# Two blocks of a sequence model: a weight remainder on VectorE, modulation loads two turns later, modulation sums behind the softmax divisions

## What is computed

```python
def first_block(x, ...):
    proj = rms_norm(x, g_mix) @ w_in                       # 1024 -> 4352
    xa = depthwise_conv(u_a, conv_a_w, conv_a_b, 2)
    y_a = (rglru(xa, forward) + rglru(xa, backward)) @ p_a # 1280 wide
    y_b = (block_diag(multiscale_pool(u_b), w_pool, b_pool) * pool_scale) @ p_b
    x = x + (gates_a * y_a + gates_b * y_b) @ w_out
    up = depthwise_conv(rms_norm(x, g_ffn) @ w_up, conv_f_w, conv_f_b, 1)
    x = x + (gelu(up[..., :2816]) * up[..., 2816:]) @ w_down
    return rms_norm(x, g_final)

def second_block(x, c, ...):
    mod = silu(c) @ w_mod + b_mod                          # 1024 -> 6 x 1024
    shift1, scale1, gate1, shift2, scale2, gate2 = split(mod, 6)
    u = rms_norm(h, norm1_g) * (1 + scale1) + shift1
    xs, q, ckv, qi, ki, wi, ga, gb = split_cols(u @ w_in)
    y_ssm = s5_branch(xs, ...)         # state space scan, gelu, gated product
    y_att = dsa_branch(q, ...) @ w_attn_proj  # 8 heads, top-128 keys per query
    h = h + gate1 * ((sigmoid(ga) * y_ssm + sigmoid(gb) * y_att) @ w_out)
    u2 = rms_norm(h, norm2_g) * (1 + scale2) + shift2
    h = h + gate2 * ((silu(u2 @ w_gate) * (u2 @ w_up)) @ w_down)   # 2816 wide
    return rms_norm(h, final_g)
```

## Time and profile before

| | |
|---|---|
| time, median of three runs | 1467.01 us (1464.62, 1467.01, 1467.63) |
| the profiled execution's own time | 1468.92 us |
| its span, first to last instruction | 1467.6 us |
| TensorE busy | 1450.2 us, 99% |
| VectorE busy | 888.4 us, 61% |
| ScalarE busy | 787.8 us, 54% |
| GpSimd busy | 173.0 us, 12% |
| mean granted clock of TensorE | 0.996 of full speed |
| HBM read and written | 177.62 and 17.83 MB |

### The profile page before, as it was taken

The page is one execution under the profiler, slowest core; times in us unless marked ns, Lnnn a source line. Parts: engine busy times, 40 slices in busy tenths (PEclk is TensorE's granted clock), DMA queues, the critical chain, the costliest instruction groups (busy, mean ns, idle before and its releaser), DMA issues.

```text
span 1467.6 us, 18322 instructions
## 1 busy us (share of the span) xinstructions
PE 1450.2 (99%) x6992; PEld 1190.5 (81%) x6992; DVE 888.4 (61%) x1623; ACT 787.8 (54%) x1082; POOL 173.0 (12%) x183
## 2 busy tenths in 40 slices
PE   9999999999999999999999999999999999999998
PEld 8887788888888788888888877776878888888887
DVE  6879854365595859476477668847876343333332
ACT  6699898745665556543444565586356222222221
POOL 1111111111111111100002421121010000000000
PEclk9999999999999999999999999999999999999999
DMA  8876888899999798883348666895467433333321
GB/s 260 190 193 161 205 190 200 193 318 292 305 262 273 183 243 224 207 259 122 108 165 280 198 165 167 205 337 201 141 155 222 150 107 109 87 101 100 101 72 58
DMA packets 86935, 275.42 MB, mean 188 GB/s; under 512 B 10096, under 2 KB 14448, under 8 KB 86848
## 3 DMA queue, kind: packets, MB, share of 16 engines
q1 hardware_dynamic: 62256, 190.95, 38.8%
q0 software_dynamic: 21344, 77.67, 27.8%
q10 hardware_dynamic: 3248, 5.64, 1.1%
HBM read 177.62 MB, written 17.83 MB: 133 GB/s over the span
## 4 chain that ended last, share of the span: by engine, by line
PE 86%; ACT 5%; DVE 5%; DMA 2%; issue 1%; SPq 0%; DVEq 0%; ACTq 0%
PE ps L725 27%; PE ps L728 26%; PE ps L726 26%; DMA wlo<-raw 2%; ACT whi L1222 1%; ACT wlo L1231 1%; DVE pl_f L2119 1%; ACT pl_f L1345 1%; PE ps L1071 1%; PE ps L845 0%; PE ps L960 0%; DMA tab<-pl_f 0%; PE ps L979 0%; DVE pl_f L2142 0%; PE ps L834 0%
## 5 line engine op out<-in xcount | busy, mean ns | idle before, releaser
L725 PE MATMUL ps<-pl_r,whi 128*128 128x512 f32 x1954 | 767.3, 393 | 8.4 <-DMA wlo<-raw 4.1
L726 PE MATMUL ps<-pl_r,wlo 128*128 128x512 f32 x1954 | 762.4, 390 | 0.0
L728 PE MATMUL ps<-pl_r,whi 128*128 128x512 f32 x1954 | 762.2, 390 | 0.1
L725 PEld LDWEIGHTS ps<-pl_r,whi 128*128 128x128 f32 x1954 | 367.7, 188 | 91.3 <-issue 7.9
L728 PEld LDWEIGHTS ps<-pl_r,whi 128*128 128x128 f32 x1954 | 367.9, 188 | 77.6 <-DVE pl_r L2168 0.5
L726 PEld LDWEIGHTS ps<-pl_r,wlo 128*128 128x128 f32 x1954 | 367.8, 188 | 75.2 <-issue 0.5
L1222 ACT ACTIVATE whi<-raw 128x1024 fp32r<-128x1024 f32 x246 | 259.3, 1054 | 189.8 <-PE ps L728 149.8
L2541 POOL DMA_DIRECT2D wlo<-raw x148 | 128.4, 868 | 838.0 <-ACT wlo L1231 697.7
L2231 DVE TENSOR_TENSOR wlo<-raw,whi 128x1024 fp32r<-128x1024 f32 x97 | 119.9, 1241 | 92.6 <-ACT whi L1222 92.6
L1231 ACT ACTIVATE wlo<-raw 128x1024 fp32r<-128x1024 f32 x148 | 154.8, 1046 | 0.0
L2495 DVE TENSOR_TENSOR pl_f<-ps,pl_f 128x512 f32<-128x512 f32 x20 | 13.8, 692 | 133.3 <-PE ps L728 133.3
(11 more groups left out here) (300 smaller groups left out, 1180.2 us busy)
## 6 DMA issues: line engine op xcount, KB each, us to landing
raw<-in_w SPq DMA_DIRECT2D x245, 512.0 KB, 4.6
wlo<-raw POOLq DMA_DIRECT2D x148, 512.0 KB, 6.5
pl_f<-in_mod SPq DMA_DIRECT2D x48, 512.0 KB, 7.9
pl_f<-tab SPq DMA_DIRECT2D x12, 512.0 KB, 7.2
xs<-pl_f SPq DMA_DIRECT2D x16, 256.0 KB, 7.9
tab<-pl_f SPq DMA_DIRECT2D x8, 512.0 KB, 6.1
pl_f<-xs SPq DMA_DIRECT2D x16, 256.0 KB, 5.8
spill<-pl_f ACTq DMA_DIRECT2D x16, 256.0 KB, 5.0
```

The lines of the kernel that those rows point to most:

```text
L725: matmul(out, wh, sr(pair, kk, "hi"), start=start, stop=False)
L726: matmul(out, wl, sr(pair, kk, "hi"), start=False, stop=False)
L728: mm = matmul(out, wh, sr(pair, kk, "lo"), start=False, stop=stop)
```

## The change

Three parts. First, unit 2 joins the list `BY_VECTOR`: VectorE makes its remainder in the head, by an added call between `add_squares(0, 3)` and `add_squares(4, 5, 6, 7)`, and ScalarE's negative and GpSimd's adding DMA for this unit go. On TensorE the second partial sum goes from behind block (4, 0) to behind (4, 2), and the rows from (4, 2) to (5, 0). Second, the six modulation loads of the first feed-forward are issued at j = 4 to 9 and not at j = 2 to 7. Third, in the second mixer seven modulation sums leave turns 3, 5 and 6 of `glu` and stand behind the second head's divisions of head pairs 1, 2 and 3 (two, two and three).

```diff
-BY_VECTOR = [*range(115, 138), *range(140, 146), *range(169, 177), 185, *range(188, NUNIT)]
+BY_VECTOR = [2, *range(115, 138), *range(140, 146), *range(169, 177), 185, *range(188, NUNIT)]
...
-    first(FIRST_IN, "v1", {(3, 1): lambda: sums([1], 0, last=4), (4, 0): lambda: sums([1], 4, last=4),
-                           (4, 2): lambda: to_rows(1)})
+    first(FIRST_IN, "v1", {(3, 1): lambda: sums([1], 0, last=4), (4, 2): lambda: sums([1], 4, last=4),
+                           (5, 0): lambda: to_rows(1)})
...
     add_squares(0, 3)
+    remainder(2, slice(0, 1024), ("raw", 2), ("w_hi", 2), ("w_lo", 2))
     add_squares(4, 5, 6, 7)
...
-    units = Units(NLO, BY_VECTOR[0])
+    units = Units(NLO, BY_VECTOR[1])
...
                     ts(f, f, sm("rsm", c), None, ALU.mult).then_inc(*done.tick(("p_part", hh, t)))
+                if h:
+                    mod_step((0, 2, 2, 3)[hp])
                 yield
...
-            mod_step((0, 0, 1, 2, 3, 2, 3, 2)[m])
+            mod_step((0, 0, 1, 0, 3, 0, 0, 2)[m])
...
-        if 2 <= j < 8:
+        if 4 <= j < 10:
             load_mod()
```

## The result

The changed kernel takes **1456.84 us** (median of four runs, 1456.21 to 1457.38) against 1466.34 beside it (1464.62 to 1467.63): a ratio of 0.9927, 95% interval 0.991 to 0.9944. The forecast was 1455.6, between 1453.0 and 1461.5. Beside two later repeats on other chips the ratio is 0.9923 both times. The profiled execution took 1457.31, 11.6 us less than the one before; the sum in the prediction was 12.3.

The account below looks back on a forecast made before the run. TensorE bounds the kernel, busy 1450.2 of 1467.6 us; gains come only from its waits and half rate. 2.9 + 4.0 + 5.4 = 12.3 us off 1468.92 gives 1456.6, less half of 1.9: 1455.6, range 1453.0 to 1461.5.

Parts of the forecast that it names:

- The three places: Head, first feed-forward near 500 us, second mixer near 1019 us: TensorE waits, then runs at half clock rate.
- Part 1, 2.9 us: Head: unit 2's remainder on VectorE removes TensorE's 1.4 us wait and the half rate behind it; gain 2.9 us.
- rival (b): Head's gain given back in part by unit 7, the sums at (4,2) or the clock: 1 to 2 us, 1457.4; 14%.
- 1.7 us of half rate: Work lost in 3.4 us at half clock rate behind a TensorE stall, in each of three places; 5.1 us in all.
- Part 2, 4.0 us: First feed-forward: later modulation loads remove TensorE's 2.3 us wait at 500 us and 1.7 us of half rate.
- rival (a): First feed-forward: a table store lands late, in 10.53 us instead of 7.12, the wait returns, no gain there: 1459.6; 15%.
- Part 3, 5.4 us: Second mixer: sums moved behind the divisions remove TensorE's waits at transposes and scores and the half rate; gain 5.4 us.
- Pair 3: Second mixer: with three sums away, pair 2's remainder L1683 starts 3.4 us earlier and everything behind it follows; gain 3.4 us.
- pairs 1 and 2: Second mixer: the transposes' 1.2 us wait for divisions and 0.5 us of slower running both go; gain 1.7 us.
- The cover of 0.8 behind the divisions: Second mixer: three sums cost 3.5 us where VectorE stood 4.34 us before L1683, so they are covered by 0.8.
- spoke against part 3: Second mixer: divisions near GpSimd's product could be blocked by the shared port, up to 1.1 us late; sum 0.4 less.
- (d): First feed-forward: store lands over 10.6 us later, so the kernel is slower; a 20 us landing gives about 1469; 2%.

Follow-up runs that it names:

- one_turn: The changed kernel with the first feed-forward's modulation loads one turn later (j = 3 to 8) than originally, not two; 1456.54 us, ratio 0.9923 to the kernel before.

## Why the prediction was right, and where it was not

- **The three places** were the right ones, and each wait went by the mechanism named. The sum in the profile was 12.3 for 11.6 measured; without the 2.2 given back in that execution it would have been 13.8.
- **Part 1, 2.9 us: too large.** With the other parts it is 1.7 by the times, which is rival (b) in its size. The stall goes as worked out, but the 1.7 us of half rate that the step counted in full comes only in some executions: of the four traces with the old head only the one before has it, and their stall is 0.56, 0.68, 1.40 and 1.49 us. Two steps were wrong besides. "With the sums left at (4,0) TensorE would have stood there": the additions end at 19.4, not 19.8, and it doesn't stand. And the cost "at nothing" on ScalarE and GpSimd missed what is queued behind ScalarE's wait for the moved sum, the rounding of unit 4; the next late unit is 4 and not 7.
- **Part 2, 4.0 us:** 4.4 between the traces, 2.9 alone by the times (1.6 to 4.3 by the interval). The 1.7 of half rate, counted in full, may be the difference again. The first store landed after 6.57 us with the modulation load issued 0.48 behind it, as taken: rival (a) did not come at that store. The rule of the Trainium skill that was weighed there (DMA: Bandwidth & Descriptors, Queues, rings and completion order) agrees: in nine traces with that load 0.4 to 1.3 us behind the store it landed after 6.57 to 7.36 us, in three without it after 6.75 to 7.14. Another store landed after 9.07 in one execution; the prediction hadn't looked at that one. That SyncE would not be held was wrong, 8.1 us remain, and `one_turn` shows that it doesn't matter.
- **Part 3, 5.4 us:** 5.6 alone by the times, 6.0 between the traces. Pair 3 was put at 3.4 and is 3.8 by the times and 3.6 between the traces; pairs 1 and 2 were put at 1.7 and are 2.4 between the traces. Part of that is the transposes themselves, which took 3.07 us for each pair and now take 2.89 and 2.35: 0.9 for both where the step had 0.5. The cover of 0.8 behind the divisions is 0.81. Behind it TensorE gave back 1.0: the transposes L1071 of pair 3 now come as early as the divisions allow and take 3.06 where they took 2.35.
- **The rule of the Trainium skill** that spoke against part 3 (SBUF — State Buffer, Who interferes with whom) had nothing to act on: no division ran beside GpSimd's product in the changed kernel, so no run here tests it for divisions. The nearest began 0.15 us behind the product's end, at 975.4. The three sums left in turn 4 still show the slowing that the prediction read in the earlier trace rows, in the changed kernel:

```profile
982.19 2.18 POOL L2629 TENSOR_TENSOR pl_f<-pl_f,pl_f 128x512 f32<-128x512 f32 x1 [4.04 <-DVE pl_f L2445]
```

```profile
983.15 2.30 DVE L2120 CUSTOM_DVE_ANT_0 pl_f<-pl_f,pl_f 128x1024 f32<-128x1024 f32 x1
```

- **From profile to median** 0.95 was taken off; 0.47 it was (1457.31 less 1456.84). The 1.9 us of before may in good part be the half rate, which that execution had in all three places; no run separates it. The forecast came 1.2 us too low by this and by the sum's 0.7.
- **That it came so close is in part luck.** Part 1 was too large and part 3 too small, and the half rate that the sum counted in three places is rarer in the other traces (one stall of eight). The two repeats of the changed kernel, 1456.59 and 1456.02, lie 1.0 and 0.4 above the forecast.
- **Two times of rivals were off by their own terms:** 3.4 and 1.7 us on top of 1455.6 give 1460.7 for rival (a), not 1459.6, and a landing of 20 us gives about 1470 for (d), not 1469. The forecast and its range don't hang on them.

## What to carry to other kernels

A stall of TensorE costs its own length where it stands; the half rate behind it comes only in some executions, and the profiled execution that showed it in every place was dearer than the median. Gains don't add along a stream: a lead won early is lost at the next wait that another engine's chain sets, so that later wait must go first, or with it. When a matmul that an engine waits for is moved later, look at all that stands in that engine's queue behind its wait, not only at who reads the result.

## What the runs showed of the hardware

The same stall of 1.55 us, in the same place, was followed by full rate in one execution and by 6.7 us at half rate in another. Waits of 0.47 to 0.75 us at one place were followed by half rate in one trace of fourteen. One 512 KB store of SyncE's queue, the third of a table, landed after 4.93 to 6.77 us in thirteen traces and after 9.07 in one, and whether GpSimd's adding DMA had been issued just before it doesn't tell which. A modulation sum on VectorE (1.21 us alone) and GpSimd's product (1.28 alone) took 2.30 and 2.18 when they met.
